# Split fp32 products that walk their moving columns backwards, in a two-block transformer kernel

## The reference

```python
def reference(x, c, ctx, c_ctx, ...):
    x = first_block(x, c, ctx, c_ctx, ada_w, ada_b, norm_g, ffn_w_in, ffn_w_out, da_w_in, ...)
    return second_block(x, w_in_2, ...)

def first_block(...):                      # DEPTH = 2
    h, hc = x, ctx
    for i in range(DEPTH):
        m, mc = adaln(c, ...), adaln(c_ctx, ...)           # silu(c) @ (1024 x 9216)
        h  = half_ffn(h, m, 0, ...)                        # 1024 -> 2 x 2816 -> 1024, swiglu
        hc = half_ffn(hc, mc, 0, ...)
        u, uc = modulated_norm(h, ...), modulated_norm(hc, ...)
        y, yc = diff_attention_mixer(u, uc, ...) if i == 0 else gqa_axial_mixer(u, uc, ...)
        h = gated_residual(h, y, ...)
        h = half_ffn(h, m, 6, ...)                         # and the same for hc in layer 0
    return h

def hybrid_layer(x, w_in, ...):            # second_block: two of these, then an rms norm
    p = rms_norm(x, norm_w) @ w_in                         # 1024 -> 9180 columns
    y_a = dsa_attention(...); y_b = stick_breaking_attention(...); y_c = mlstm_chunkwise(...)
    proj = einsum('bsgc,gcd->bsgd', branches, w_branch)    # 3 x (512 -> 1024)
    mixed = sum(sigmoid(merge) * proj)
    return x + mixed @ w_out
```

## Time and profile before

| | |
|---|---|
| median of three runs | 2419.73 us (2419.41 to 2421.0) |
| span of the profiled execution | 2419.5 us |
| TensorE products (PE), busy | 2384.9 us, 99%, 14712 of them |
| stationary loads (PEld), busy | 2059.6 us, 85% |
| VectorE, busy | 1600.1 us, 66% |
| ScalarE, busy | 1063.2 us, 44% |
| granted TensorE clock, mean | 0.997 |
| DMA | 346.53 MB, mean 143 GB/s |

### The profile page before, as it was taken

One profiled execution on the slowest core, in us unless ns is written; L12 is line 12 of the kernel. 1 busy time (PEld: TensorE's weight loads), 2 busy tenths in 40 slices (PEclk: granted clock), 3 DMA queues, 4 the chain that ended last, 5 costly groups with the idle time before them and its releaser, 6 DMA issues.

```text
span 2419.5 us, 36353 instructions
## 1 busy us (share of the span) xinstructions
PE 2384.9 (99%) x14712; PEld 2059.6 (85%) x14712; DVE 1600.1 (66%) x2899; ACT 1063.2 (44%) x1882; POOL 0.2 (0%) x4
## 2 busy tenths in 40 slices
PE   9999999999999999999999999999999999999998
PEld 5888888976788888888888888899998998999997
DVE  7776775477587677377623357655586776877767
ACT  4222324455552223252223245644556556555663
POOL 0000000000000000000000000000000000000000
PEclk9999999999999999999999999999999999999999
DMA  6554552211125455215522212245534443444432
GB/s 275 207 195 188 202 198 70 88 53 53 71 91 197 186 198 203 87 55 207 207 107 90 102 70 88 111 157 181 191 142 157 175 140 127 167 169 158 157 123 88
DMA packets 48408, 346.53 MB, mean 143 GB/s; under 512 B 5361, under 2 KB 5489, under 8 KB 6769
## 3 DMA queue, kind: packets, MB, share of 16 engines
q1 hardware_dynamic: 48242, 344.21, 38.3%
HBM read 343.14 MB, written 1.05 MB: 142 GB/s over the span
## 4 chain that ended last, share of the span: by engine, by line
PE 92%; DVE 5%; ACT 2%; issue 1%; DMA 0%; SPq 0%; DVEq 0%; ACTq 0%
PE ps L484 26%; PE ps L485 25%; PE ps L486 25%; PE ps L826 1%; PE ps L828 1%; PE ps L827 1%; DVE w_lo L2119 1%; PE ps L873 1%; PE ps L1030 1%; PE ps L654 1%; ACT w_hi L1430 1%; PE ps L679 1%; PE ps L1056 1%; PE ps L859 1%; PE ps L608 1%
## 5 line engine op out<-in xcount | busy, mean ns | idle before, releaser
L1430 ACT ACTIVATE w_hi<-ring 128x1024 fp32r<-128x1024 f32 x494 | 523.4, 1060 | 1052.5 <-PE ps L486 988.9
L2119 DVE TENSOR_TENSOR w_lo<-ring,w_hi 128x1024 fp32r<-128x1024 f32 x494 | 603.5, 1223 | 422.8 <-ACT w_hi L1430 419.5
L484 PE MATMUL ps<-u_hi,w_hi 128*128 128x512 f32 (+1 forms) x1856 | 656.8, 354 | 4.8 <-DVE u_lo L2192 2.3
L485 PE MATMUL ps<-u_lo,w_hi 128*128 128x512 f32 (+1 forms) x1856 | 648.6, 349 | 0.0
L486 PE MATMUL ps<-u_hi,w_lo 128*128 128x512 f32 (+1 forms) x1856 | 648.4, 349 | 0.0
L484 PEld LDWEIGHTS ps<-u_hi,w_hi 128*128 128x128 f32 x1856 | 348.4, 188 | 60.9 <-issue 7.7
L485 PEld LDWEIGHTS ps<-u_lo,w_hi 128*128 128x128 f32 x1856 | 348.5, 188 | 47.3 <-issue 0.5
L486 PEld LDWEIGHTS ps<-u_hi,w_lo 128*128 128x128 f32 x1856 | 348.6, 188 | 45.5
L484 PE MATMUL ps<-uh,w_hi 128*128 128x256 f32 x1136 | 321.9, 283 | 2.9 <-DVE w_lo L2119 1.7
L2107 DVE CUSTOM_DVE_ANT_0 waste<-ring,condb,cols 128x1024 f32<-128x1024 f32 x260 | 322.3, 1279 | 0.1
L486 PE MATMUL ps<-uh,w_lo 128*128 128x256 f32 x1136 | 315.4, 278 | 0.0
(11 more groups left out here) (364 smaller groups left out, 2686.6 us busy)
## 6 DMA issues: line engine op xcount, KB each, us to landing
ring<-in_wk SPq DMA_DIRECT2D x317, 1024.0 KB, 4.8
mix<-in_wk SPq DMA_DIRECT2D x3, 1024.0 KB, 16.2
yT<-in_wk SPq DMA_DIRECT2D x2, 1024.0 KB, 7.8
hT<-in_x SPq DMA_DIRECT2D x1, 2048.0 KB, 13.1
htabs<-in_htabs SPq DMA_DIRECT2D x1, 1088.0 KB, 7.3
out_t<-uT SPq DMA_DIRECT2D x2, 512.0 KB, 2.6
trig<-in_trig SPq DMA_DIRECT2D x3, 256.0 KB, 7.5
wuk<-in_uk SPq DMA_DIRECT2D x2, 256.0 KB, 5.1
```

What stands on the lines that cost most here:

```text
L484: mm(bank, hi, x_hi, start=first, stop=False, skip_group_check=skip)
L485: mm(bank, hi, x_lo, start=False, stop=False, skip_group_check=skip)
L1430: f(half_hi(K, 0, HALF), ringed(n, K % 2 * HALF, (K % 2 + 1) * HALF), ACT.Copy).then_inc(whi_ready, 1)
L2119: tt(half_lo(K, 0, HALF), ringed(HALF_SLOT[K], K % 2 * HALF, (K % 2 + 1) * HALF), half_hi(K, 0, HALF).bitcast(F32), ALU.subtract).then_inc ...
```

## The change

The split products take the last column of the moving operand first and write the last column of the output first, and so on down to column 0. Both sides are turned, so each output column gets what it got before. The stationary operand, the number of instructions, their order, and all waits are the same.

```diff
@@ def three(bank, hi, lo, x_hi, x_lo, first, last, skip=False):
+                bank, x_hi, x_lo = bank[:, ::-1], x_hi[:, ::-1], x_lo[:, ::-1]
                 mm(bank, hi, x_hi, start=first, stop=False, skip_group_check=skip)
                 mm(bank, hi, x_lo, start=False, stop=False, skip_group_check=skip)
                 return mm(bank, lo, x_hi, start=False, stop=last, skip_group_check=skip)
@@ def values(...):
-                        mm(bank, x_h, half_hi(h, n, n + 256), start=k == 0, stop=False)
-                        mm(bank, x_l, half_hi(h, n, n + 256), start=False, stop=False)
-                        last = mm(bank, x_h, half_lo(h, n, n + 256), start=False, stop=k == KC - 1)
+                        back, w_h, w_l = bank[:, ::-1], half_hi(h, n, n + 256)[:, ::-1], half_lo(h, n, n + 256)[:, ::-1]
+                        mm(back, x_h, w_h, start=k == 0, stop=False)
+                        mm(back, x_l, w_h, start=False, stop=False)
+                        last = mm(back, x_h, w_l, start=False, stop=k == KC - 1)
```

## The result

| | before | after |
|---|---|---|
| median of four runs | 2419.57 us (2418.47 to 2421.0) | 2465.01 us (2464.56 to 2465.24) |
| span of the profiled execution | 2419.5 us | 2462.8 us |
| ratio of times | | 1.0188, 95% interval 1.0174 to 1.0203 |

The change makes the kernel 1.9% slower. I had forecast 2359 us, and 2440 us was the end of my range.

What follows compares the result with a forecast made beforehand. The prediction took TensorE's issue of split products as the bound. From a span of 2419.5 us it took off 43 us for 512 columns and 17 us for 256, together 60, giving 2359 us, range 2310 to 2440.

Steps and rivals of the forecast that it cites:

- What bounds the kernel, and what a nanosecond is worth: TensorE's issue of 12744 split products sets the end; each nanosecond per product is worth 12.7 us.
- No instruction, wait or order changes; the write order is seen by nobody: Same instructions, waits and semaphores; no engine reads a product's bank before its group ends; only TensorE time per product can change.
- The value that I take: Turning the moving read against the stationary load frees every split product: 220 and 113.3 ns, 60 us less, chance 0.45.
- The 220 ns for 512 columns: Split products of 512 columns: 113.3 ns plus 107 for 256 more beats, instead of 228.9 ns.
- The 43 us that I took off for 512 columns: Gain on 4824 split products of 512 columns going from 228.9 to 220.0 ns: 43 us.
- the 17 us for 256 columns: Gain on half of the 256-column split products, 3960, each 4.4 ns quicker: 17 us.
- Covered supply: Weights are made and streamed fast enough for a quicker TensorE: 1.22 us of VectorE per 2.7 us half slot.
- locked worse: Rival: the two reads meet on every product, quick 256-column stretches go to 117.5 ns; 17 us more, 2437 us, chance 0.10.
- lost run: Rival: each descending column becomes an access of its own, 430 and 215 ns per product; 4170 us, chance 0.18.
- The range: 2310 us, all excess over plain matmuls gone, to 2440 us, just past 2437; leaves out only a 0.18 chance.
- the bound above of 1750 us: Upper bound on split products: a second beat per column adds 970 us with 512 columns and 784 with 256.

Runs made afterwards that it cites:

- write_back: Kernel before with only the output of the split products written last column first, reads forwards; 2419.95 us, ratio 0.9995.
- the place experiments: Forward-only kernels, TensorE alone or the kernel before, with moving or stationary tiles shifted in SBUF; in the kernel, 32 bytes left free behind the weights lost 1.8%.
- the 256 places: TensorE alone, all forwards, moving and stationary tiles each shifted 0 to 60 columns in steps of 4; 512 columns took 226.7 to 236.8 ns.
- shift80: Kernel before, all forwards, with weights and activations together 80 bytes later; 226.7 ns with 512 columns, 118.3 ns in most stretches with 256.
- micro2: TensorE alone, 55 forms with stationary tiles shifted or fewer stationary or moving columns; backwards with 2 stationary columns 233.3 ns (512 columns) and 117.8 ns (256).
- read_back: Kernel before with only the moving operands of all split products read last column first, output written forwards; 2466.0 us, ratio 1.0182.

## Why the prediction was wrong

- *What bounds the kernel, and what a nanosecond is worth*: right. The distances of the split products grew by 47 us and the span by 43, and the 3.6 us between them are within what the other work differs by from trace to trace. No engine or transfer hid a part of the loss.
- *No instruction, wait or order changes; the write order is seen by nobody*: right (same counts; write_back 0.9995).
- *The value that I take*: here it failed. From two paces on equal tiles I concluded that the moving read and the load of the next stationary operand lock to each other, which the place experiments support for the forward walk, and then that turning one of them would free all products. The second step had no row under it: nothing said which way the two reads walk, nor that a turned walk has a free state. No run found one: no full backward walk took less than 233.3 or 117.7 ns. The helper's products now hold one pace whatever came ahead of them, 233.3 and 120.0, and the value tiles' 117.8, and this is the far end, not the near one. The 220 ns for 512 columns had no row either, and none of the 256 places forwards has less than 226.7. The 43 us that I took off for 512 columns were 20.7 us added, the 17 us for 256 columns 22.8 added and 3.4 more for the value tiles.
- *Covered supply*: not put to the test by after. In shift80, with 512 columns at 226.7 ns, no new wait came.
- *The rival "locked worse"*: the nearest to what happened, and mis-sized. It had the quick stretches of 256 columns go from 113.3 to 117.5, 17 us in all; they went to 120.0, those that stood at 117.8 went there as well, and the 512-column ones, which I had left alone, went from 228.9 to 233.3. Its mechanism, a meeting of the two reads on every product, has by micro2 no part in the loss of 512 columns and up to 2.2 ns in that of 256.
- *The rival "lost run"*: its sign came (233.3 and 120.0 are more than its 229 and 115.6, and read_back puts the loss on the read), its price did not: a full backward walk is 4.4 ns above forwards, not 201. A second beat for each column is thus not what a descending read takes, and blocks of up to 4 columns may run either way at no cost (228.9 ns).
- *The range* ended at 2440 since I took the trace's slower pace for the worst there is. A pace between 229 and 430 ns for 512 columns was nowhere weighed; the bound above of 1750 us was priced as one case with nothing between.

The cause is shown as far as this: the descending read of the moving operand, with no other engine in it, at the place that this kernel's tiles have. What stays open is why it costs what it does (4.4 ns at 512, 6.5 at 448, nothing at 320 columns), what part the stationary load has in it at 256 columns, and why blocks of 16 columns cost most. The direction of the stationary operand's read wasn't tried.

## What to carry to other kernels

Where one engine is the bound, measure a product by the distance from start to start in steady stretches: differences of 4 ns in 229 and 2 to 7 in 115, invisible in busy shares, were 1.9% of the kernel. Two paces on equal work show that something besides the work decides; they don't show that a change of order leads to the better one, and such a bet needs a small kernel of the one operation, which here separated what the whole kernel could not. Walk the moving operand upwards where its tiles stand well, and if a few tenths of a per cent matter, try the placement of its tiles against the stationary ones; both the loss and the gain there come without any change of instructions.

## What the runs showed of the hardware

- The moving operand of an fp32r product is read at a cost that depends on its order: where the tiles stand as in this kernel, descending order costs 4.4 ns in 229 (512 columns), 2.2 to 6.7 in 113 to 118 (256 columns) and nothing at 128, 192 and 320 columns; where the forward walk takes 233.4 by its place, descending order costs nothing more; inside 4 columns, and between blocks of 64 columns or more, the order is free. The order of the PSUM write is free (0.9995).
- A forward split product of 512 columns took 226.7 to 240 ns at one clock, mostly by the addresses of its two operands; at one place, both shifted by 16, two stretches differed (228.9 and 233.4). A moving operand shifted by a single column (4 bytes) took 240 ns. A shift by 64 columns (256 bytes) gives the pace of no shift, 228.9.
- With 128 or 192 moving columns a split product takes 111.7 ns in either direction, and no steady stretch of split products had less.
- After a plain product of 128 columns the first split product holds TensorE for about 200 ns with 256 columns and 316 with 512, some 85 ns more than the next ones; after one of 256 columns it was 308 and 423.
